# Layer 2's output gates computed by features, with the attention turned first and multiplied from a bank, and a new order of the output opening

## What is computed

```
q, k, v, gate = split(h @ w_in)                     # q, k rotated by position
a = softmax(q1 k1) - lam * softmax(q2 k2)           # per head, causal
o = rmsnorm(a @ v, subln) * (1 - lambda_init)       # 8 heads of 128 features
y = o.reshape(B, S, 1024) * silu(gate)
h = h + rmsnorm(y @ w_out, norm_post)
```

## Time and profile before

| | us |
|---|---|
| median of 3 runs | 2646.74 (2646.5 to 2647.12) |
| the profiled execution | 2646.64 |
| its span in the trace | 2645.3 |

### The profile page before, as it was taken

One profiled execution on the slowest core, in us unless ns is written; L12 is line 12 of the kernel. 1 busy time (PEld: TensorE's weight loads), 2 busy tenths in 40 slices (PEclk: granted clock), 3 DMA queues, 4 the chain that ended last, 5 costly groups with the idle time before them and its releaser, 6 DMA issues.

```text
span 2645.3 us, 35469 instructions
## 1 busy us (share of the span) xinstructions
PE 2611.0 (99%) x13561; PEld 2123.6 (80%) x13561; DVE 1247.6 (47%) x2448; ACT 1038.3 (39%) x1939; POOL 1145.5 (43%) x890
## 2 busy tenths in 40 slices
PE   8999999999999999999999999999999999999998
PEld 6888878778778777777888888887777688888887
DVE  3535354554566365446255423265544624542426
ACT  4343434443546344453333424234435233342422
POOL 4434334425342344333464444454332446444443
PEclk9999999999999999999999999999999999999999
DMA  6434343433332332234352333324222435233321
GB/s 196 129 102 122 101 116 112 112 112 100 100 96 73 103 96 80 80 91 141 122 166 80 113 98 101 96 82 133 80 80 76 152 108 177 80 112 96 96 96 64
DMA packets 215121, 282.22 MB, mean 107 GB/s; under 512 B 22016, under 2 KB 155620, under 8 KB 214184
## 3 DMA queue, kind: packets, MB, share of 16 engines
q1 hardware_dynamic: 214952, 279.95, 34.5%
HBM read 246.28 MB, written 16.84 MB: 99 GB/s over the span
## 4 chain that ended last, share of the span: by engine, by line
PE 94%; DVE 3%; ACT 1%; issue 1%; POOL 0%; DMA 0%; SPq 0%; ACTq 0%; DVEq 0%
PE banks L1806 37%; PE banks L1803 30%; PE banks L1799 13%; PE banks L1824 2%; PE banks L1938 1%; PE banks L1920 1%; PE banks L1863 1%; PE banks L2041 1%; PE banks L1972 1%; PE banks L2068 1%; PE banks L1906 1%; PE banks L2026 1%; PE banks L1994 1%; PE banks L2054 1%; DVE AR L2551 1%
## 5 line engine op out<-in xcount | busy, mean ns | idle before, releaser
L3177 POOL TENSOR_TENSOR WS<-WR,WS 128x512 fp32r<-128x512 f32 (+2 forms) x672 | 858.2, 1310 | 1012.9 <-ACT WS L2186 1012.9
L1806 PE MATMUL banks<-WS,UT 128*128 128x512 f32 (+1 forms) x3312 | 721.4, 370 | 5.1 <-DVE UT L2551 5.1
L1803 PE MATMUL banks<-UT,WS 128*128 128x512 f32 (+1 forms) x3024 | 707.4, 392 | 0.7 <-ACT AR L2375 0.7
L1803 PEld LDWEIGHTS banks<-UT,WS 128*128 128x128 f32 (+1 forms) x3024 | 561.8, 187 | 131.5 <-issue 14.7
L1806 PEld LDWEIGHTS banks<-WS,UT 128*128 128x128 f32 x3312 | 560.0, 188 | 117.1 <-issue 16.8
L2186 ACT ACTIVATE WS<-WR 128x1024 fp32r<-128x1024 f32 (+1 forms) x344 | 333.4, 1019 | 222.4 <-PE banks L1806 139.0
L1799 PE MATMUL banks<-UT,WS 128*128 128x512 f32 x1536 | 367.1, 394 | 0.0
L1799 PEld LDWEIGHTS banks<-UT,WS 128*128 128x128 f32 x1536 | 283.5, 188 | 64.7 <-issue 7.2
L1806 PE MATMUL banks<-WS,AT 128*128 128x512 f32 x1296 | 302.9, 393 | 3.1 <-DVE WS L2551 2.6
L1806 PEld LDWEIGHTS banks<-WS,AT 128*128 128x128 f32 x1296 | 244.5, 189 | 55.0 <-DVE WS L2551 3.0
L3175 POOL TENSOR_TENSOR WS<-WR,WS 128x512 fp32r<-128x512 f32 x128 | 181.1, 1446 | 236.6 <-ACT WS L2182 236.6
(11 more groups left out here) (225 smaller groups left out, 2526.5 us busy)
## 6 DMA issues: line engine op xcount, KB each, us to landing
WR<-in_w_in SPq DMA_DIRECT2D x112, 512.0 KB, 3.6
WR<-in_w_up SPq DMA_DIRECT2D x88, 512.0 KB, 3.5
WR<-in_dil_w_in SPq DMA_DIRECT2D x64, 512.0 KB, 3.8
WR<-in_w_down SPq DMA_DIRECT2D x40, 512.0 KB, 3.7
WR<-in_diff_w_in SPq DMA_DIRECT2D x32, 512.0 KB, 3.7
WR<-in_dil_w_in SPq DMA_DIRECT2D x32, 256.0 KB, 3.9
AR<-AF SPq DMA_DIRECT2D x128, 64.0 KB, 2.7
AR<-AF SPq DMA_DIRECT2D x64, 128.0 KB, 2.5
```

What stands on the lines that cost most here:

```text
L1803: mm = pe.matmul(B[bank][0:c, :], w[part][:, kk, g * P:g * P + c], act[:, other, kk, :], start=start, stop=stop)
L1806: mm = pe.matmul(B[bank][:, off:off + n], act[:, other, before_k + kk, g * P:g * P + P], w[part][:, kk, :], start=start, stop=stop)
L3177: ge.tensor_tensor(slot(i, 1)[:, s], raw(i)[:, s], slot(i, 0)[:, s].bitcast(F32), ALU.subtract).then_inc(lo_p.sem, 1)
```

## The change

The gates of layer 2 are computed by `feature_major`. Step `times` now begins on PE: it waits for the norm of the heads, turns the four 128x128 blocks of X for one chunk of 128 features into a corner bank, and DVE multiplies 0.5 * gate by that bank into X, by features; the corner bank is let go by this multiply. Step `chunk` has no part on PE any more: ACT copies out of X, and DVE subtracts with X as its source. The opening's list is: chunk 4, chunk 5, l2o0, `times` (last tile, first half), l2o1, `times` (second half), chunk 6, chunk 7, and the last four matmul steps as before. The number of matmul columns, transposes, copies and multiplies is the same; the DMAs are the same.

```diff
     def gates(self, name, done, late, gated):
-        across = self.feature_major if name == "l1g" else self.token_major
...
-            yield from across(f"{name}{j}", deal)
+            yield from self.feature_major(f"{name}{j}", deal)
...
-        for x in late:
-            self.step("times", *x)
         self.by_blocks([f"l2o{j}" for j in range(4)], self.residual("l2o"),
-                       self.opening([("chunk", "l2g", c) for c in range(4, 8)]))
+                       [("chunk", "l2g", 4), ("chunk", "l2g", 5), (0, 0, 4), ("times", *late[0]), (1, 0, 4),
+                        ("times", *late[1]), ("chunk", "l2g", 6), ("chunk", "l2g", 7),
+                        (2, 0, 2), (3, 0, 2), (2, 2, 4), (3, 2, 4)])
...
             elif kind == "chunk":
                 chunk_hi.plan(tuple(a))
-                done = chunk_lo.plan(tuple(a))
-                if a[0] == "l2g":
-                    k = takes_corner(("chunk", *a))
-                    chunked.plan(tuple(a))
-                    freed[k] = done
+                chunk_lo.plan(tuple(a))
...
             elif kind == "times":
-                timed.plan((a[0], a[1]))
+                done = timed.plan((a[0], a[1]))
+                if tiles[a[0]][0][:2] == "l2":
+                    k = takes_corner(("times", a[0], a[1]))
+                    chunked.plan((a[0], a[1]))
+                    freed[k] = done
...
-            if name[:3] in ("l1w", "l2g"):
+            if name[:3] == "l1w":
                 return 112
...
-            return bank[:, :], AT[:, 0, c, :], AT[:, 1, c, :]
+            return (X[:, :, c * P:c * P + P], *(AT[:, q, c, :].rearrange("p (b t) -> p b t", b=NB) for q in range(2)))
...
-                elif kind == "chunk" and a[0] == "l2g":
-                    tag, c = a
-                    pe.wait_ge(timed.sem, timed.at[index[f"{tag}{c // 2}"], 1])
-                    k = bank6["chunk", tag, c]
-                    pe.wait_ge(*before["chunk", tag, c])
+                elif kind == "times" and tiles[a[0]][0][:2] == "l2":
+                    i, half, j = a
+                    c = 2 * j + half
+                    pe.wait_ge(head_normed.sem, head_normed.at[j])
+                    k = bank6["times", i, half]
+                    pe.wait_ge(*before["times", i, half])
                     for b in range(NB):
                         mm = pe.transpose(B[k][:, b * P:b * P + P], X[:, b, c * P:c * P + P], IDN)
                     mm.then_inc(chunked.sem, 1)
...
+                    se.wait_ge(timed.sem, timed.at[index[f"{tag}{c // 2}"], c % 2])
...
+                    elif c > 3:
+                        se.wait_ge(summed.sem, summed.at["2", N2 - 1])
...
                     else:
-                        ve.wait_ge(head_normed.sem, head_normed.at[j])
-                        d = X[:, 2 * half:2 * half + 2, 256 * j:256 * j + 256]
-                        tv = tv.rearrange("p (b n) -> p b n", b=2)
-                    ve.scalar_tensor_tensor(d, tv, 0.5, d, ALU.mult, ALU.mult).then_inc(timed.sem, 1)
+                        ve.wait_ge(chunked.sem, chunked.at[i, half])
+                        c = 2 * j + half
+                        d = X[:, :, c * P:c * P + P]
+                        tv, bank = (view(v, (NB, P)) for v in (tv, B[bank6["times", i, half]][:, :]))
+                        ve.scalar_tensor_tensor(d, tv, 0.5, bank, ALU.mult, ALU.mult).then_inc(timed.sem, 1)
```

More of the change, by code:

```diff
@@ L1253, in gate_bank @@
         def gate_bank(i, half):
-            return order.bank[i, half if tiles[i][0][:3] == "l1g" else 2 * half][0]
+            return order.bank[i, half][0]
         def blocks_in(unit, what):
@@ L1716, in turn_dst, with chunk_io @@
             return AT if tag[0] == "o" else UT
-        def chunk_io(tag, c, bank):
+        def chunk_io(tag, c):
             if tag == "l1g":
@@ L1785, in tensor @@
                         pe.wait_ge(prod_lo.sem, prod_lo.at[int(name[1]), 10, 1, 1])
-                    by_feature = name[:3] == "l1g" or name[:4] in ("m0ik", "m1ik", "m0gq", "m1gq", "m0gb", "m1gb", "m0ga", "m1ga", "m0pa",
+                    by_feature = name[:3] in ("l1g", "l2g") or name[:4] in ("m0ik", "m1ik", "m0gq", "m1gq", "m0gb", "m1gb", "m0ga", "m1ga", "m0pa",
                                               "m1pa", "m0pg", "m1pg") or name[0] == "f" and name[2] in "ab"
@@ L2212, in scalar @@
                     tag, c = a
-                    src, d, _ = chunk_io(tag, c, B[bank6["chunk", tag, c]] if tag == "l2g" else None)
+                    src, d, _ = chunk_io(tag, c)
                     if c == 0:
@@ L2216, in scalar @@
                             se.wait_ge(*there(index[f"l1{name}23" if tag == "l1g" else f"l2{name}3"]))
+                    se.wait_ge(timed.sem, timed.at[index[f"{tag}{c // 2}"], c % 2])
                     if tag == "l1g":
-                        se.wait_ge(timed.sem, timed.at[index[f"l1g{c // 2}"], c % 2])
                         if c in (4, 5):
@@ L2222, in scalar @@
                             se.wait_ge(summed.sem, summed.at["1", N1 - 2])
+                    elif c > 3:
+                        se.wait_ge(summed.sem, summed.at["2", N2 - 1])
                     if tag == "l2g":
-                        se.wait_ge(chunked.sem, chunked.at[tag, c])
                         if c == 0:
@@ L2308, in scalar @@
                     i, half, j = a
-                    se.wait_ge(proj.sem, proj.at[i, half if tiles[i][0][:3] == "l1g" else 2 * half + 1])
+                    se.wait_ge(proj.sem, proj.at[i, half])
                     if j > 0:
@@ L2593, in vector @@
                     tag, c = a
-                    src, d_hi, d_lo = chunk_io(tag, c, B[bank6["chunk", tag, c]] if tag == "l2g" else None)
+                    src, d_hi, d_lo = chunk_io(tag, c)
                     ve.wait_ge(chunk_hi.sem, chunk_hi.at[tag, c])
@@ L2719, in vector @@
                         d = XT[:, 2 * j + half, :]
+                        ve.scalar_tensor_tensor(d, tv, 0.5, d, ALU.mult, ALU.mult).then_inc(timed.sem, 1)
                     else:
-                        ve.wait_ge(head_normed.sem, head_normed.at[j])
-                        d = X[:, 2 * half:2 * half + 2, 256 * j:256 * j + 256]
-                        tv = tv.rearrange("p (b n) -> p b n", b=2)
-                    ve.scalar_tensor_tensor(d, tv, 0.5, d, ALU.mult, ALU.mult).then_inc(timed.sem, 1)
+                        ve.wait_ge(chunked.sem, chunked.at[i, half])
[3 more added lines that the diff above has]
+                        ve.scalar_tensor_tensor(d, tv, 0.5, bank, ALU.mult, ALU.mult).then_inc(timed.sem, 1)
                 elif kind == "lambda":
```

## The result

The changed kernel took 2652.27 us (median of 14 runs, 2650.37 to 2655.16) against 2646.88 for the kernel before (14 runs, 2645.05 to 2650.44): a ratio of 1.0019, 95% interval 1.0011 to 1.0027. It is slower, by about 5 us where 4.3 had been summed, and the interval lies on both sides of the 0.2% that had been set as the bound. Each ratio in this text is to runs of the kernel before that were taken alongside. The profiled execution has a time of 2651.38 us and a span of 2650.1.

A forecast was written before the change was run, and what follows sets the result against it. PE (TensorE), busy for nearly the whole span, was taken as the bound. Stage +5.3 and opening -1.0 summed to +4.3 us, so 2651.0 us (+0.16%), with eight in ten from 2645.5 to 2654.5.

The forecast's parts named there:

- signs of being wrong: Stage staying at 70 us, opening ending under 15.5 us after last attention output, or six 512-column matmuls not taking 1.47.
- Form: Layer 2's gate matmuls, 12 of 256 columns becoming 6 of 512 per step: 0, with 0.6 us either way.
- Stage: Layer 2's first gate matmul to first output matmul: transposes and corner-bank waits, less vanished gaps, +5.3 us (4.9 to 5.7).
- Gate 0: First half: a turn waits for its corner bank until DVE's late multiply, starting at about 796.2; +1.65 us.
- Gate 2: First half: transposes wait 2.3 to 3.1 us for the head norm, next turn 0.65 more; taken 3.4.
- The four other sets: The three sets after gate 0's first half, and gate 2's second half: +0.3 us of waits, bounds 0 and 0.8.
- The subtraction's price: DVE's subtraction in step chunk, now of two SBUF tensors: between 0.7 and 2.1 us, 1.6 where POOL runs.
- Opening: From E, the last attention output's end, to the sixth matmul step: -2.3 to -0.5 us, taken -1.0.
- dear end: Opening with subtractions slowed and POOL's quarters 1.5 us: sixth step ends 17.7 us after last attention output, -0.5 us.
- The clock falls: Rival: clock drops behind gate 2's wait or in the opening, about 1.7 us each; 2652.6 or 2654.2; chance 0.36.
- The banks don't bite: Rival: DVE reaches gate 0's multiply and gate 2's norm sooner, stage waits go: -2.4, 2644.4 us; chance 0.10.
- Half of it: Rival: DVE is ahead by gate 2, that wait 1.2 instead of 3.4 us: 2648.5; chance 0.12.

The follow-up runs named there:

- e2: Kernel before with only layer 2's gates computed by feature_major (multiply takes the gate in the wrong layout): 2646.64 us, ratio 0.9998.
- e1: Changed kernel with layer 2's times steps, and chunks 0 to 3, issued three matmul steps later: 2646.9 us, ratio 1.0003.
- e5: Changed kernel with POOL's passes over five weight tiles (l2g2, l2g3, l2o0, l2o2, l2o3) only writing zeros: 2645.13 us, ratio 0.9990.
- e3: Changed kernel with chunks 4 and 5 issued ahead of the split of l2o2 in the opening: 2653.77 us, ratio 1.0027.
- e4: Changed kernel with times three steps later and chunks 4 and 5 ahead of the split of l2o2: 2647.99 us, ratio 1.0007.
- e7: Changed kernel with times three steps later, chunks 4 and 5 first, opening reordered, l2o3's low part by DVE instead of POOL: 2646.26 us, ratio 0.9995.
- e6: Kernel before with POOL's passes over five weight tiles (l2g2, l2g3, l2o0, l2o2, l2o3) only writing zeros: 2647.3 us, ratio 1.0000.

## Why the prediction was right

The mechanism was the one forecast, and none of the prediction's signs of being wrong came. By its own steps:

- **Form, 0.** Held (e2), and each step takes 1.47 us.
- **Stage, +5.3.** 5.2 by the trace. Gate 0: 1.46 us for 1.65, at 796.21 for "about 796.2". Gate 2: 2.76 and 0.51, 3.3 for 3.4; the subtraction queued ahead of the norm slowed by 1.0, where 0.8 had been weighed, but the norm itself took 2.35 instead of 2.81. The four other sets waited for nothing of note, where 0.3 had been put, and a set cost 0.44 to 0.53 instead of 0.38. e1 and e5 bear out the mechanism from both ends: the waits go when the sets come later, and also when DVE comes sooner.
- **The subtraction's price, 1.6.** 1.58 to 1.77 where POOL ran, 0.75 where it didn't, as the prediction's rows on either side had it. That its partner matters, and how, e5's rotation shows: 1.29 us for two, with a POOL that only writes at work from its start to its end. The Trainium skill (SBUF — State Buffer, "SBUF: two separate sides") says this too: a DVE operation with two SBUF inputs is kept out only by a GpSimd operation that reads SBUF. The 1.29 of e5 agrees. e5's subtractions, 1.42 for two, say less: POOL writes beside them for only 0.4 us.
- **Opening, -1.0.** -0.6: the sign was right, and so was POOL as the next in line; the size was at the dear end of the range (-0.5). What was mis-sized is POOL: it started l2o2 5.2 us after E, its quarters took 1.48 us instead of the 1.26 of the earlier trace rows, and its pass over l2o3 ended 17.0 us after E where 15.2 had been put by the cheap price. The third step came at E + 10.1, the dear forecast being 9.9. The prediction had the dear sum (sixth step done at E + 17.7; it was at 876.15 + 1.36, E + 17.6) and chose a value between. With POOL reading throughout, and the only row of that kind at the dear price, the dear end was the one to take.
- **Rivals.** "The clock falls" did not show behind the new gaps in the changed kernel's profile, where the windows say 1.00; but in e3 it did, behind the same gap of 2.76, for 0.75 us. The median of 2652.27 is a little above the forecast without falls (2649 to 2652) and near the 2652.6 of one fall. The changed kernel's runs at a mean granted clock of 0.999 took 2650.37 to 2651.38 us, those at 0.997 or less 2652.22 to 2655.16, so falls go with the long runs. But the kernel before spreads likewise (2644.51 to 2645.67 at 0.999 and 2648.14 to 2650.41 at 0.997 or less, in the runs beside e1), and whether any of it falls behind the new gaps is not shown. The price of a fall is 1.6 by the earlier trace rows (4.57 - 2 x 1.47), which the prediction gives as 1.7 and adds as 1.6. "The banks don't bite" has its condition, less of POOL's work beside DVE, in e5, and the change is faster there by 2.6 us, where 2.4 had been reckoned. The sum agrees, its parts don't: the stage keeps 1.4 us of loss (two sets and 0.45 + 0.51 of waits, less the old gap) where none was left in the reckoning, and the opening gives 4.0 instead of 2.3. "Half of it" didn't happen: DVE was not ahead by gate 2.

The sum was 0.5 short of the profiled execution's span, and 0.4 of that is the opening. That the spans of these two executions can be compared so closely is luck: in each the clock fell once ahead of the first gate matmul, at different gaps (last section). The rest to the median is within what single executions differ by.

## What to carry to other kernels

A step that PE takes over from a slower engine's tail also takes over that engine's lateness: before moving a transpose or a turn ahead of an elementwise operation, put its due time beside the end of what it reads, as the two sets that came too early here cost 4.7 us of waiting, and with all of them three places later the stage loses 0.7 us instead of 5.2. When a wait is taken away, follow the remaining chain from its own start (here norm, split on ACT, POOL's two passes) to see whether it is any shorter; if not, PE only waits later, and one long wait in place of two short ones can cost the clock as well, as in e3 and e4. Price elementwise operations of two SBUF inputs by rows in which POOL is reading, and POOL by the same rows.

## What the runs showed of the hardware

That POOL slows DVE had been expected; not that it depends on what POOL does. The rotation, 128x512 by 128x512 from SBUF, takes 0.65 us a piece beside a memset (e5) and 1.7 beside a `tensor_tensor` (the changed kernel). POOL's quarters in the opening take 1.26 us in the kernel before, where DVE subtracts from banks, and 1.48 in the changed kernel, where it subtracts from SBUF. The operations with one input in a bank stay as they were: the multiplies of the opening take 1.27 us for two with POOL at work (869.84 in the changed kernel).

The granted clock behind gaps of the same length differs from one execution to the next. One gap in layer 2's attention, ahead of all the edits, is 2.66 us in all nine kernels. PE's timeline of the changed kernel has it so, where the earlier trace rows has it before:

```profile
746.52 2.07 PE L1994 MATMUL banks<-AR,AF 128*128 128x128 f32 x8 [2.66 <-ACT AF L2368]
```

with these windows behind it, as in the earlier trace rows,

```profile
746.50:747.50 1.00, 0.98 (x4) 0.98 (x5) 0.00 (x0) 0.00 (x0) 1.00 (x2) 0.52 0.00 0
747.50:748.50 1.00, 1.00 (x7) 1.00 (x6) 0.00 (x0) 0.00 (x0) 0.63 (x1) 0.50 0.30 56
```

and PE's timeline of e7 so:

```profile
746.94 1.16 PE L2003 MATMUL banks<-AR,AF 128*128 128x128 f32 x8 [2.66 <-ACT AF L2377]
```

The clock fell behind it in after, e2, e4, e5 and e6, and didn't in before, e1, e3 and e7. To the next gap it is 3.66 or 3.67 us where the clock held (751.83 - 748.16 before), 5.07 to 5.28 where it fell (751.80 - 746.52 after), and 6.17 in e4. The gaps of layer 1's output projection differ in the same way: behind one of 2.47 to 2.60 us near 579 the clock fell in before, e1 and e4 and not in e5 and e7, and behind one of 1.83 near 580 or 581 it fell in e2 and not in e3 and e6.

These falls are most of what differs ahead of the first gate matmul, which starts anywhere between 783.20 and 788.26. From the start of layer 1's output projection's row of 24 matmuls (568.04 to 569.39) to that first gate matmul, the same instructions take 214.6 us in e3 and e7, where no such fall shows; 216.0 to 216.4 in before, after, e1, e5 and e6, with one; and 217.8 in e2 and 220.0 in e4, with two.

Behind the edits it is no different. The clock fell behind the gap of 2.26 us in e1 and not in after, and behind the one of 2.76 in e3 and not in after; behind the gaps of 3.42 to 3.73 in the opening it fell in all five kernels that have one. What a fall costs depends on what comes next: 1.4 to 2.5 us at the gap of 2.66, 0.75 in the stage of e3, and nothing in e1, where PE would have waited for POOL's pass anyway (16.24 us from E to the sixth step, against 16.23 in after without the fall).
